# Gate and up products of the experts as three rounded products, with the weights split inside the block loop and loaded in 8 KB runs

## What is computed

```
def swiglu(x, w_gate, w_up, w_down):
    return (jax.nn.silu(x @ w_gate) * (x @ w_up)) @ w_down
...
    def block(args):
        tok, e = args
        return swiglu(h_pad[tok], w_gate[e], w_up[e], w_down[e])
...
    out = out.reshape(n_rows, D) * row_w[:, None]
    return jax.ops.segment_sum(out, row_tok, num_segments=T + 1)[:T]
```

## Time and profile before

| | |
|---|---|
| median of 3 runs | 2447.08 us (2446.58 to 2448.67) |
| the profiled execution | 2447.2 us, its span 2445.6 us |
| PE / PEld busy | 2171.7 us (89%) / 1337.6 us (55%) |
| DVE / ACT / POOL busy | 771.2 us (32%) / 441.7 us (18%) / 327.1 us (13%) |
| DMA | 423.48 MB, mean 173 GB/s |
| stage `experts` | about 1222 to 2375 us |

### The profile page before, as it was taken

The page is one execution under the profiler, slowest core; times in us unless marked ns, Lnnn a source line. Parts: engine busy times, 40 slices in busy tenths (PEclk is TensorE's granted clock), DMA queues, the critical chain, the costliest instruction groups (busy, mean ns, idle before and its releaser), DMA issues. The chain is left out here.

```text
span 2445.6 us, 34914 instructions
## 1 busy us (share of the span) xinstructions
PE 2171.7 (89%) x9591; PEld 1337.6 (55%) x9592; DVE 771.2 (32%) x1738; ACT 441.7 (18%) x796; POOL 327.1 (13%) x331
## 2 busy tenths in 40 slices
PE   3899995999997996989869999999999999999960
PEld 3899995676564663446334444445444444444430
DVE  3101114433264322323123333333333333333325
ACT  4111101443012110111201111111111111111112
POOL 0101001000000000000012222222222222222210
PEclk9899998999898998978979999999999999999985
DMA  5211110111323654232159888989998888679836
GB/s 209 70 43 51 45 34 17 38 49 39 103 74 111 226 180 176 103 130 80 70 187 309 249 255 244 343 258 342 344 324 272 243 245 242 197 199 288 252 69 218
DMA packets 276030, 423.48 MB, mean 173 GB/s; under 512 B 12431, under 2 KB 208259, under 8 KB 275986
## 3 DMA queue, kind: packets, MB, share of 16 engines
q1 hardware_dynamic: 242290, 300.06, 36.2%
q0 software_dynamic: 32528, 118.60, 18.0%
q10 hardware_dynamic: 1168, 4.23, 0.4%
HBM read 345.37 MB, written 77.49 MB: 173 GB/s over the span
## 5 line engine op out<-in xcount | busy, mean ns | idle before, releaser
L1639 PE MATMUL bank<-wexp,xT 128*128 x1488 | 659.9, 596 | 16.0 <-issue 14.0
L1639 PEld LDWEIGHTS bank<-wexp,xT 128*128 128x128 f32 x1488 | 276.0, 190 | 334.8 <-issue 334.1
L1676 PE MATMUL bank<-wexp,hTe 128*128 x736 | 331.1, 592 | 0.0
L1605 POOL DMA_INDIRECT acc_d<-ob,ixs x92 | 145.0, 1576 | 782.3 <-DVE ob L1775 751.8
L524 PE MATMUL bank<-hT,wg 128*128 128x344 f32 x768 | 237.8, 464 | 7.5 <-ACT gst L535 7.3
L1676 PEld LDWEIGHTS bank<-wexp,hTe 128*128 128x128 f32 x736 | 132.7, 190 | 132.0 <-issue 132.0
L426 PE MATMUL bank<-hT_hi,w_hi 128*128 128x344 f32 x576 | 187.5, 325 | 14.9 <-DVE w_lo L493 14.9
L524 PEld LDWEIGHTS bank<-hT,wg 128*128 128x128 f32 x768 | 144.9, 193 | 96.7 <-ACT gst L535 16.7
L1716 DVE TENSOR_TENSOR oh<-iota,posm 128x1152 bf16 x96 | 130.4, 1358 | 202.5 <-issue 202.5
L426 PE MATMUL bank<-hT_hi,w_lo 128*128 128x344 f32 x576 | 185.4, 322 | 0.0
L426 PE MATMUL bank<-hT_lo,w_hi 128*128 128x344 f32 x576 | 184.8, 321 | 0.0
(11 more groups left out here) (303 smaller groups left out, 2104.0 us busy)
## 6 DMA issues: line engine op xcount, KB each, us to landing
wexp<-in_w_exp_gate SPq DMA_DIRECT2D x64, 1024.0 KB
wexp<-in_w_exp_up SPq DMA_DIRECT2D x64, 1024.0 KB
wexp<-in_w_exp_down SPq DMA_DIRECT2D x64, 1024.0 KB
wada<-in_w_ada SPq DMA_DIRECT2D x12, 2048.0 KB, 10.7
w_raw<-in_w_in SPq DMA_DIRECT2D x28, 512.0 KB, 3.8
gates_d<-gst POOLq DMA_DIRECT2D x48, 172.0 KB, 2.1
gate<-gates_d SPq DMA_DIRECT2D x16, 516.0 KB, 5.3
wg<-in_w_in SPq DMA_DIRECT2D x16, 512.0 KB, 4.0
```

Source lines behind the costliest of these rows:

```text
L1605: pool.indirect_dma_start(out=acc_d, out_offset=bass.IndirectOffsetOnAxis(ap=ixs[b][:, 0:1], axis=0), in_=ob[:, b, :], in_offset=None, com ...
L1639: return pe.matmul(banks[0][:], xT[:, b, k, :], wexp[:, bass.ds(slot, 1), k, :].rearrange("p a n -> p (a n)"), start=(k == 0), stop=(k == ...
L1676: last = pe.matmul(banks[4 + half][:], hT[:, f, :], wexp[:, bass.ds(slot, 1), KD + 2 * f + half, :].rearrange("p a n -> p (a n)"), start=( ...
```

## The change

- `up` does 24 float32r matmuls of 512 columns in place of 8 float32 ones: hi·hi, hi·lo, lo·hi.
- `take`: ACT rounds both halves of the transposed rows into `x_hi`, and DVE writes both halves of `x_lo`.
- In every block ACT rounds the gate and up weights (`round_weights(i+2)`, two operations on 128x2048), and DVE writes what is left of them (`rest_of_weights(i+2, x)`, two subtractions on 128x2048) over the raw weights in the ring. This is done in every block, a second block of the same expert too: there it is done on the next expert's weights, and DVE's result goes to a slot that is free. Two more columns of the table say which.
- The whole of `ob` is now ACT's. DVE's order in a block is `weight`, `place`, `to_gather`, rest 0, `gate`, rest 1, `take`, `to_add`, `index`.
- ACT waits for `w_ok` now, in `block_of(i)` for what block i+2 needs; PE did in `block_of(i)` for block i+1.
- Gate and up weights are loaded with the inner index as p·8+k, so that each partition reads one run of 8 KB (before: 8 runs of 1 KB). For this `output_and_norm` writes `h2` with its columns permuted, from a new tile `hn`, and the router's and the shared expert's weights are loaded in the same order.
- One more load of gate and up at the end (slot 0), a larger memset of `xg`, a bound check in the gather, other places in SBUF.

```diff
--- before.py
+++ after.py
-            wexp = sb("wexp", [P, RING, KD + 4, 512], ctx=c5)
+            wdn = far("wexp_down", [P, RING, FF // P, D])
+            wexp = far("wexp", [P, RING, 2, KD * FF])
+
+            w_lo = nc.alloc_sbuf_tensor_at("wexp_lo", [P, RING, 2, KD * FF], F32R, offset=nc.sbuf_top)
+            posm = far("posm", [P, E + 1, TILES])
+            table = far("table", [1, ITEMS + AHEAD, FIELDS], I32)
...
+            trunk.close()
...
-                    s.link(dve.scalar_tensor_tensor(out=h2[0:r, t % 2, :], in0=x2[0:r, t % 2, :], scalar=st[0:r, 2:3],
+                    s.link(dve.scalar_tensor_tensor(out=hn[0:r, :], in0=x2[0:r, t % 2, :], scalar=st[0:r, 2:3],
                                                     in1=c[:, 1, :], op0=ALU.mult, op1=ALU.mult))
-                    dve.tensor_tensor(h2[0:r, t % 2, :], h2[0:r, t % 2, :], c[:, 2, :], ALU.add).then_inc(h2_ok, 1)
...
+                    dve.tensor_tensor(h2[0:r, t % 2, :].rearrange("q (k p) -> q p k", p=P),
+                                      hn[0:r, :].rearrange("q (p k) -> q p k", p=P),
+                                      c[:, 2, :].rearrange("q (p k) -> q p k", p=P), ALU.add).then_inc(h2_ok, 1)
...
-                s.link(dve.tensor_scalar(tf[:, 1, :], tf[:, 0, :], float(TILES - 1), float(P), ALU.min, ALU.mult))
-
+                s.run(dve.tensor_scalar(tf[:, 1, :], tf[:, 0, :], float(TILES - 1), float(P), ALU.min, ALU.mult))
+                s.link(dve.tensor_scalar(tf[:, 2, :], tf[:, 0, :], 1.0, None, ALU.min))
+                s.link(dve.tensor_tensor(tf[:, 2, :], tf[:, 2, :], banks[7][0:1, 0:n], ALU.add))
+                s.run(dve.tensor_scalar(table[:, :, 3], tf[:, 2, :], float(E), None, ALU.min))
+                s.run(dve.tensor_scalar(table[:, :, 2], banks[7][0:1, 0:n], float(E - 1), None, ALU.min))
...
-def load_expert(eng, a, wexp, e, slot, landed):
-
-    def src(name):
-        return a[name][0, bass.ds(e, 1)].rearrange("e (k p) n -> p (e k) n", p=P)
-
-    eng.dma_start(wexp[:, slot, 0:KD, 0:FF], src("w_exp_gate")).then_inc(landed, 16)
-    eng.dma_start(wexp[:, slot, 0:KD, FF:], src("w_exp_up")).then_inc(landed, 16)
-    eng.dma_start(wexp[:, slot, KD:, :].rearrange("p (k h) n -> p k (h n)", h=2), src("w_exp_down")).then_inc(landed, 16)
...
+def load_expert(eng, a, wexp, wdn, e, slot, landed):
+
+    for x, name in enumerate(("w_exp_gate", "w_exp_up")):
+        eng.dma_start(wexp[:, slot, x, :], a[name][0, bass.ds(e, 1)].rearrange("e (p k) n -> p (e k n)", p=P)).then_inc(landed, 16)
+    eng.dma_start(wdn[:, slot],
+                  a["w_exp_down"][0, bass.ds(e, 1)].rearrange("e (f p) n -> p (e f) n", p=P)).then_inc(landed, 16)
...
-        xT = tile("xT", [P, 2, KD, P])
+        x_hi = tile("x_hi", [P, 2, KD, P], F32R)
+        x_lo = tile("x_lo", [P, 2, KD, P], F32R)
+        w_hi = tile("wexp_hi", [P, 2, 2, KD * FF], F32R)
...
+        def source_of(u):
+
+            return u & (RING - 1)
+
+        def hi_slot(u):
+
+            return u & 1
+
+        def lo_slot(e, u):
+
+            return (e * 2 + RING - u) & (RING - 1)
+
+        def weights(w, slot, x):
+            return w[:, bass.ds(slot, 1), x, :].rearrange("p a n -> p (a n)")
...
+                sp.wait_ge(entered, E - 1)
+                for x, name in enumerate(("w_exp_gate", "w_exp_up")):
+                    sp.dma_start(wexp[:, 0, x, :], a[name][0, E - 1].rearrange("(p k) n -> p (k n)", p=P)).then_inc(slot_in[0], 16)
+                sp.wait_ge(slot_in[0], 48 * (E // RING) + 32)
+                sp.sem_inc(w_ok, 1)
...
-                pool.memset(xg[:, :, XW:XW + 1], 0.0).then_inc(pad_ok, 1)
+                pool.memset(xg[:], 0.0).then_inc(pad_ok, 1)
...
                     pool.indirect_dma_start(out=xg[:, b, 0:XW], out_offset=None, in_=xe_d,
-                                            in_offset=bass.IndirectOffsetOnAxis(ap=ix[b][:, 0:1], axis=0)).then_inc(gat[b], 16)
+                                            in_offset=bass.IndirectOffsetOnAxis(ap=ix[b][:, 0:1], axis=0),
+                                            bounds_check=ROW0 + TT - 1, oob_is_err=False).then_inc(gat[b], 16)
...
                 def up(j, b, e, c):
-                    slot = e & (RING - 1)
-
-                    def part(k):
-                        return pe.matmul(banks[0][:], xT[:, b, k, :],
-                                         wexp[:, bass.ds(slot, 1), k, :].rearrange("p a n -> p (a n)"),
-                                         start=(k == 0), stop=(k == KD - 1))
+                    slot, half = e & (RING - 1), e & 1
+
+                    def part(k, x):
+                        stat, mov, at = ((x_hi, w_hi, half), (x_hi, w_lo, slot), (x_lo, w_hi, half))[x]
+                        return pe.matmul(banks[0][:].rearrange("p (g n) -> p g n", g=2), stat[:, b, k, :],
+                                         mov[:, bass.ds(at, 1), 0:2, k * FF:(k + 1) * FF].rearrange("p a g n -> p (a g) n"),
+                                         start=(k == 0 and x == 0), stop=(k == KD - 1 and x == 2))
 
                     pe.wait_ge(xT_ok, 2 * j + 2)
+                    pe.wait_ge(wlo_ok, 2 * j + 2)
                     with pe.If(c < 1):
-                        pe.wait_ge(w_ok, e + 1)
-                        part(0).then_inc(entered, 1)
+                        part(0, 0).then_inc(entered, 1)
                     with pe.Else():
-                        part(0)
-                    for k in range(1, KD):
-                        last = part(k)
+                        part(0, 0)
+                    for k in range(KD):
+                        for x in range(3):
+                            if k or x:
+                                last = part(k, x)
                     last.then_inc(gu_ps, 1)
...
                 def take(j, b):
                     act.wait_ge(x_tp, j + 1)
-                    act.wait_ge(gu_ps, j - 1) if j is not 0 and j is not 1 else None
-                    act.activation(xT[:, b, 0:4, :].rearrange("p k n -> p (k n)"), banks[1][:], ACT.Copy).then_inc(xT_ok, 1)
+                    for half in range(2):
+                        act.activation(x_hi[:, b, 4 * half:4 * half + 4, :].rearrange("p k n -> p (k n)"),
+                                       banks[1 + half][:], ACT.Copy).then_inc(xhi_ok, 1)
 
                 def gate(j):
                     act.wait_ge(gu_ps, j + 1)
                     act.activation(sg[:], banks[0][:, 0:FF], ACT.Silu).then_inc(sg_ok, 1)
 
+                def round_weights(j):
+
+                    u = entry(act, j, 3, E)
+                    act.wait_ge(w_ok, u + 1)
+                    for x in range(2):
+                        act.activation(weights(w_hi, hi_slot(u), x), weights(wexp, source_of(u), x),
+                                       ACT.Copy).then_inc(whi_ok, 1)
+
                 take(0, 0)
+                round_weights(0)
                 take(1, 1)
+                round_weights(1)
                 gate(0)
 
                 def block_of(i, b):
                     act.wait_ge(h_tp, i + 1)
                     act.activation(hT[:].rearrange("p f n -> p (f n)"), banks[3][:, 0:FF], ACT.Copy).then_inc(hT_ok, 1)
+                    round_weights(i + 2)
                     gate(i + 1)
                     take(i + 2, b)
                     act.wait_ge(dn_ps, i + 1)
                     act.wait_ge(ixs_ok, i + 1)
-                    act.activation(ob[:, b, 0:512], banks[4][:], ACT.Copy, scale=wcol[:, b:b + 1]).then_inc(ob_ok, 1)
+                    for half in range(2):
+                        act.activation(ob[:, b, 512 * half:512 * half + 512], banks[4 + half][:], ACT.Copy,
+                                       scale=wcol[:, b:b + 1]).then_inc(ob_ok, 1)
...
                 def take(j, b):
-                    dve.wait_ge(x_tp, j + 1)
-                    dve.tensor_copy(xT[:, b, 4:8, :].rearrange("p k n -> p (k n)"), banks[2][:]).then_inc(xT_ok, 1)
+                    for half in range(2):
+                        at = slice(4 * half, 4 * half + 4)
+                        dve.wait_ge(xhi_ok, 2 * j + half + 1)
+                        dve.tensor_tensor(x_lo[:, b, at, :].rearrange("p k n -> p (k n)"), banks[1 + half][:],
+                                          x_hi[:, b, at, :].rearrange("p k n -> p (k n)"), ALU.subtract).then_inc(xT_ok, 1)
+
+                def rest_of_weights(j, x):
+
+                    e, u = entry(dve, j, 2, E - 1), entry(dve, j, 3, E)
+                    dve.wait_ge(whi_ok, 2 * j + x + 1)
+                    dve.tensor_tensor(weights(w_lo, lo_slot(e, u), x), weights(wexp, source_of(u), x),
+                                      weights(w_hi, hi_slot(u), x), ALU.subtract).then_inc(wlo_ok, 1)
...
                 def block_of(i, b):
-                    dve.wait_ge(gat[1 - b], round_of(i, b) + 16 + 16 * b)
+                    dve.wait_ge(ob_ok, 2 * i + 2)
+                    weight(i + 1, 1 - b, entry(dve, i + 1, 0, E), round_of(i, b) + 16 + 16 * b)
```

(27 more changed lines are left out.)

42 lines of the change are left out of this document (18 added, 24 removed).

## The result

The changed kernel takes **2640.69 us** (median of 4 runs, 2635.07 to 2642.3), the kernel before in the runs beside it 2447.88 (4 runs, 2446.58 to 2449.26). The ratio is 1.078, with an interval from 1.0768 to 1.08: slower by 193 us. The forecast was 2603 us, in a range from 2540 to 2715. The profiled execution is the fastest of the four, 2635.07 us.

A forecast was written before the change was run, and what follows sets the result against it. PE was taken to bound the kernel before, DVE's in-order queue the changed one: 91 blocks x (13.6 - 11.98) = 147 us, plus 9 us of small parts, makes 156; 2447 + 156 = 2603 us, range 2540 to 2715.

The forecast's parts named there:

- DVE as the new bound: Block loop: DVE's in-order queue sets the pace at 13.6 us a block, between 12.9 and 15.5; chance 0.77.
- The subtractions: DVE's two weight subtractions of 2048 elements per block: 2.3 us each, 4.6 together, of 8.66 us executed.
- Reads ahead of the first subtraction: Two table reads behind `place` and `to_gather` on DVE: partly hidden, 0.7 us a block sticking out.
- Reads of the second one: Two table reads behind rest 0 and `gate` on DVE: hidden, costing nothing; 2 us more if not covered.
- Loop, `If` and the other reads: DVE's block loop, `If`, and reads for `weight` and `place`: 4.0 us a block, down from 4.14.
- The small parts: Outside the steady loop: `xg` memset +2.4, prologue subtractions and reads +6, last `ob` on ACT +1; 9 us together.
- the memset: Start of the kernel: `xg` memset grows to 2178 columns, about 2.5 us, with DVE waiting, so +2.4 us.
- PE: `up` takes 24 matmuls at 0.234 us, 5.6 us instead of 6.9: 1.3 us less, PE's block work 10.4 us.
- The rival on the other side: PE stays the bound and gains its 1.3 us, needing a DVE period under 10.4 us: 2312 us; chance 0.05.
- The clock: Rival: PE's gaps lower its granted clock, `gate` comes late to DVE, 1.4 us a block: 2731 us; chance 0.09.
- Weights late: Rival: ACT stands 3 us on weight loads for about 36 of 64 experts, 108 us on top: 2711 us; chance 0.05.

The follow-up runs named there:

- short_rest: Changed kernel with DVE's two weight subtractions per block cut to 64 of 2048 columns and `w_lo` products reading `w_hi`: 2431.02 us, ratio 0.9927.
- extra_read: Changed kernel with one more, unused table read into a register ahead of `place` in each block: 2679.67 us, ratio 1.0948.
- reads_once: Changed kernel with the two table entries for both subtractions read once per block, ahead of the first, rather than twice: 2610.74 us, ratio 1.0666.
- runs_only: Kernel before with only the 8 KB weight runs, permuted `h2` and its reordered readers; float32 products, no split: 2449.58 us, ratio 1.0009.

## Why the prediction was right, and where it was off

- **DVE as the new bound.** Right: `short_rest` takes 210 us away, leaving out two thirds of `up` only 33, and in `extra_read` a bare read shows its 0.72 us ahead of `oh`.
- **The subtractions**: 2.3 us each forecast, 2.29 measured. `x_lo` 1.28 for 1.38. Executed in all 8.24 rather than 8.66: instructions that follow each other directly overlap by 0.08 us, which a sum of durations misses.
- **Reads ahead of the first subtraction**: this is the term that was most mis-sized. 0.7 us were said to stick out, 1.42 do. In a quiet block it is 1.17; the other 0.25 are the 18 blocks with slow reads, which the prediction had at nothing.
- **Reads of the second one**: said to be hidden, 2 us if not. Right in 51 of 72 blocks and wrong in 21, 0.26 us a block. The prediction itself says that no row shows a read running past an unmet wait, and yet counts `gate`, which begins with such a wait, as cover. It does cover them when `sg` is early.
- **Loop, `If` and the other reads**: 4.0 forecast, 2.19 + 1.51 = 3.70 measured.
- Together 13.56 forecast, 13.94 measured. 0.38 x 91 = 35 us, nearly the whole difference to 2603. That the sum came so close is in part luck: the reads were 0.98 us too low, the executed time and the loop 0.72 too high. The small parts were 9 us and measured 6.4; the memset took 1.91 us.
- **PE**: the products of `up` start every 0.23 us, as carried on in a line from the earlier trace rows. Its gain of 1.3 us a block, with the clock at its upper level, bought nothing.
- **The rival on the other side** needed a DVE period below 10.4 us. `short_rest` has 11.78, and 10.4 only in its shortest blocks: with two full subtractions on DVE it was out of reach.
- **The clock**: it falls, and costs little. The timeline of PE in the changed kernel:

```profile
1712.58 0.79 PE L1679 MATMUL bank<-wexp_hi,x_hi 128*128 x1 [3.25 <-DVE x_lo L1788]
...
1713.62 0.63 PE L1679 MATMUL bank<-wexp_hi,x_lo 128*128 x1
1714.04 0.63 PE L1679 MATMUL bank<-wexp_hi,x_hi 128*128 x1
...
1715.72 0.40 PE L1679 MATMUL bank<-wexp_lo,x_hi 128*128 x1
1715.95 0.40 PE L1679 MATMUL bank<-wexp_hi,x_lo 128*128 x1
```

After 3.25 us of standing still the products come every 0.42 us, the 1.2 GHz level (granted clock 0.50 from 1713 to 1715), and from 1715.72 every 0.23 us again. `up` takes 7.27 us up to `sg` where it takes 6.1 at the full clock. In this block `sg` still ends at 1720.24, before the first subtraction starts (1720.83), so the reads behind the wait start in time. Where it ends later they don't, and that is the 0.26 us a block above. So the rival had the fall right, and also that `gate` comes late to DVE; its price was 1.4 us a block, five times too high, because `sg` can end up to 0.4 us after the start of the first subtraction before anything is lost, and beyond that only the excess counts.
- **Weights late**: ACT waits 52.7 us for them in 72 blocks, 0.7 us a block, where the rival had 3 us for 36 experts of 64. Little of it reaches DVE: where the rounding ends DVE's wait, the idle time is no longer than in a quiet block.

## What to carry to other kernels

An engine's busy share leaves out what its queue does between instructions. Here 4 of 12 us a block were loop, `If` and table reads in DVE's queue, and with them two subtractions of 2.3 us were more than a block had room for. Add them up before you give an engine more work, and count which of them the new work hides. A table read is hidden only if no unmet wait stands ahead of it in the queue: so read ahead of the wait, as `reads_once` does (30 us). And a group of the profile can hold two instructions of a block: look at the timeline before you put its idle time down to one of them. Work that is moved between VectorE and GpSimd is only moved if the instructions beside it don't both read SBUF.

## Not expected of the hardware

- A subtraction of POOL with SBUF inputs shuts out a DVE operation with two SBUF inputs, even one of a single column: 0.16 us become 2.71. With an input in PSUM it runs beside, 0.17 us.
- A table read of 0.30 us takes 0.76 to 1.18 us now and then: ahead of the first subtraction in 18 of 72 blocks. The cause is open.
- A table read does not start ahead of a wait that stands before it in the queue: in the block shown the first read started as `sg` ended, and in all 21 blocks with a late `sg` the subtraction behind the two reads started 2.10 to 2.28 us after its end.
- In the changed kernel the three weight loads issued from 1713.55 us on take 0.33, 0.38 and 0.38 us to issue, where the last one of an expert took 6.66 before. In `runs_only` it is 0.33 to 0.53 us between 1690 and 1740 us, and nothing is gained by it.
